# Further tokens turned ahead of the tables, gathers behind the last full table block, nine rows taken ahead of the loop

## What is computed

```python
s = einsum('bshcd,hckd->bshck', q, peer_keys)      # 8 heads, 2 halves, 128 keys
sv, si = top_k(s, 16)                              # then the best 16 of 16 x 16 sums
idx, g = expert numbers, softmax of the best 16    # 8 x 16 = 128 experts per token
act = gelu(einsum('thkd,td->thk', peer_u[it], xt)) * gt
out = einsum('thk,thkd->td', act, peer_v[it])      # 16384 experts, rows of 2048
```

## Time and profile before

| | |
|---|---|
| median of 3 runs | 3809.42 us (3808.86 to 3809.46) |
| span of the profiled execution | 3806.1 us (the page gives no other time of it) |
| PE busy | 3758.1 us, 99% |
| DVE, ACT, POOL busy | 2363.5, 1263.3, 1697.3 us |
| granted PE clock, mean | 0.996 |
| gathers' queue | 303.22 MB, 22.4% of the DMA engines' span |
| queue of SP | 492.34 MB, 35.8% |

### The profile page before, as it was taken

One profiled execution on the slowest core, in us unless ns is written; L12 is line 12 of the kernel. 1 busy time (PEld: TensorE's weight loads), 2 busy tenths in 40 slices (PEclk: granted clock), 3 DMA queues, 4 the chain that ended last, 5 costly groups with the idle time before them and its releaser, 6 DMA issues. The chain is left out here.

```text
span 3806.1 us, 56597 instructions
## 1 busy us (share of the span) xinstructions
PE 3758.1 (99%) x20173; PEld 3449.1 (91%) x20173; DVE 2363.5 (62%) x4027; ACT 1263.3 (33%) x1638; POOL 1697.3 (45%) x1449
## 2 busy tenths in 40 slices
PE   7999999999999998999999999999999999999999
PEld 5778778888888887889999999999999999999999
DVE  5382453000010207886968888888887888888887
ACT  3443453333333323224652222222222222222221
POOL 0444434444444662444015545545553555555223
PEclk9999999999999999999999999999999999999999
DMA  6223112222222322234569989889888898989777
GB/s 199 96 85 105 67 56 99 97 90 99 99 96 91 144 99 104 105 105 151 215 260 312 323 326 326 320 328 333 321 313 286 311 335 314 329 319 338 278 295 248
DMA packets 187946, 800.97 MB, mean 210 GB/s; under 512 B 21024, under 2 KB 59944, under 8 KB 134440
## 3 DMA queue, kind: packets, MB, share of 16 engines
q1 hardware_dynamic: 99776, 492.34, 35.8%
q0 software_dynamic: 83872, 303.22, 22.4%
q10 hardware_dynamic: 4184, 4.01, 0.5%
HBM read 762.39 MB, written 37.09 MB: 210 GB/s over the span
## 5 line engine op out<-in xcount | busy, mean ns | idle before, releaser
L791 ACT ACTIVATE w_hi<-ring 128x1024 fp32r<-128x1024 f32 (+1 forms) x499 | 564.5, 1136 | 1097.4 <-PE bank L1766 744.1
L637 POOL TENSOR_TENSOR p_lo<-ring,p_hi 128x512 fp32r<-128x512 f32 x432 | 563.4, 1305 | 674.3 <-ACT p_hi L791 588.7
L1766 PE MATMUL bank<-h_hi,w_hi 128*128 128x368 f32 (+1 forms) x2304 | 782.2, 339 | 16.4 <-DVE w_lo L1586 7.5
L1766 PE MATMUL bank<-h_lo,w_hi 128*128 128x368 f32 (+1 forms) x2304 | 775.8, 337 | 0.0
L1766 PE MATMUL bank<-h_hi,w_lo 128*128 128x368 f32 (+1 forms) x2304 | 775.6, 337 | 0.0
L1766 PE MATMUL bank<-act_hi,w_hi 128*128 128x368 f32 x2048 | 674.0, 329 | 0.1
L1766 PE MATMUL bank<-act_hi,w_lo 128*128 128x368 f32 x2048 | 673.9, 329 | 0.0
L1766 PE MATMUL bank<-act_lo,w_hi 128*128 128x368 f32 x2048 | 673.9, 329 | 0.0
L757 POOL DMA_INDIRECT grow<-v_rows,g_col x288 | 383.0, 1330 | 512.9 <-DVE g_acc L1621 387.3
L1586 DVE TENSOR_TENSOR w_lo<-ring,w_hi 128x1024 fp32r<-128x1024 f32 x448 | 546.2, 1219 | 81.9 <-ACT w_hi L791 62.7
L791 ACT ACTIVATE p_hi<-ring 128x512 fp32r<-128x512 f32 x464 | 292.7, 632 | 788.8 <-PE bank L1766 784.2
(11 more groups left out here) (219 smaller groups left out, 5057.7 us busy)
## 6 DMA issues: line engine op xcount, KB each, us to landing
ring<-w_exp SPq DMA_DIRECT2D x256, 1024.0 KB, 7.0
ring<-w_mix SPq DMA_DIRECT2D x64, 1024.0 KB, 4.9
tables<-wt SPq DMA_DIRECT2D x12, 2048.0 KB, 6.5
wg<-tables SPq DMA_DIRECT2D x96, 256.0 KB, 8.4
ring<-w_qk SPq DMA_DIRECT2D x20, 1024.0 KB, 4.9
ring<-w_o SPq DMA_DIRECT2D x16, 1024.0 KB, 4.9
ring<-w_pq SPq DMA_DIRECT2D x16, 1024.0 KB, 4.9
xT<-x_t SPq DMA_DIRECT2D x8, 1024.0 KB, 12.0
```

Source lines behind the costliest of these rows:

```text
L637: nc.gpsimd.tensor_tensor(p_lo[:, part, :], ring[slot][:, part, :], p_hi[:, part, :].bitcast(F32), ALU.subtract).then_inc(quarter_lo, 1)
L791: return nc.scalar.activation(out, in_, func, **kw)
L1766: return nc.tensor.matmul(out, lhsT, rhs, start=start, stop=stop)
```

## The change

1. The 16 further tokens are turned behind tile 29 (X_AFTER = 5), not in tile 44. ACT copies them to x_h and stores them itself with a DMA; x_h moves to where wt[0] will lie, so ACT waits for that store ahead of the first table copy. PE's transposes of the routes wait for x_copied.
2. Gathers no longer wait for the store of the last table: grow moves by half a KiB and its order is turned, so that grow0 and grow1 lie where only the one-hots of quarters 2 and 3 lay. DVE frees these two one quarter into the last (short) block, the other two at its end. POOL waits for nothing of x_tokens before.
3. x_tok is spread behind the first 8 turns of four rows each, that is behind row 31, not behind row 3.
4. FIRST_ROWS is (1, 2, 2, 2, 2): nine rows ahead of the loop. So three u rows are left in turn 6 instead of eight, the adds there begin two tiles sooner (14 instead of 10), LAST_ROWS sums to 16 instead of 18 and the tail has 26 instead of 28.

```diff
-TOK_AFTER, EXP_AFTER, ROUTE_AFTER = 4, 5, 6
+TOK_AFTER, X_AFTER, EXP_AFTER, ROUTE_AFTER = 4, 5, 5, 6
-TAIL_MORE = ((), (), (), (0, 3))
+TAIL_MORE = ((), (), (), ())
-FIRST_ROWS = (0, 0, 0, 2, 2)
+FIRST_ROWS = (1, 2, 2, 2, 2)
-G_TURN, T_LAST, N_TURN = 6, 5, 10
-LAST_ROWS = (1, 1, 2, 1, 1, 2, 1, 1, 2, 1, 2, 1, 0, 1, 0, 1)
+X_TURNS = 8
+G_TURN, T_LAST, N_TURN = 6, 3, 14
+LAST_ROWS = (1, 1, 1, 1, 1, 1, 1, 1, 2, 1, 2, 1, 0, 1, 0, 1)
...
-        grow = [place(f"grow{i}", 180 + 4 * i, [D // 2]) for i in range(4)]
+        grow = [place(f"grow{i}", 180.5 + 4 * ((i + 2) % 4), [D // 2]) for i in range(4)]
-        x_h = place("x_h", 188, [D])
+        x_h = place("x_h", 144, [D])
...
-            pool.wait_ge(x_copied, 4)
-            pool.dma_start(x_dram, x_h[0:NX, :]).then_inc(x_spread, 16)
-            pool.wait_ge(x_put, 32 * NS)
-            pool.wait_ge(x_spread, 16)
-            pool.wait_ge(tab_out[1], 16 * (NTB // 2))
-            pool.wait_ge(x_ready, 5)
-            pool.wait_ge(gath_free, 1)
             for b in range(2):
                 column(g_both, b, b)
-            gather(0, half_rows[0], g_both, 0)
+            with pool.Fori(0, X_TURNS) as t:
+                gather(0, half_rows[0], g_both, t)
+            pool.wait_ge(x_stored, 16)
+            pool.wait_ge(x_ready, 5)
             for k in range(NS):
                 pool.dma_start(x_tok[NX * k:NX * k + NX, :, :], x_dram.rearrange("p (a n) -> p a n", a=KC)
                                ).then_inc(x_spread, 16)
-            gather_all(0, half_rows[0], g_both, PAIRS, x_both, 1)
+            gather_all(0, half_rows[0], g_both, PAIRS, x_both, X_TURNS)
...
+                if j == X_AFTER:                                     # ScalarE, behind its part of tile 29
+                    act_e.wait_ge(x_mm, 1)
+                    for b in range(4):
+                        f(x_h[0:NX, S * b:S * b + S], bank[4 + b][0:NX, :]).then_inc(x_copied, 1)
+                    act_e.wait_ge(x_copied, 4)
+                    act_e.dma_start(x_dram, x_h[0:NX, :]).then_inc(x_stored, 16)
...
+            act_e.wait_ge(x_stored, 16)
             for b in range(2):
                 table_block(0, b, True)
...
+                    if parts < 4 and q == parts - 1:                 # VectorE, one_hots
+                        dve.sem_inc(gath_free, 2)
...
             dve.wait_ge(tab_mm, TAB_PARTS)
+            dve.sem_inc(gath_free, 2)
...
-            dve.sem_inc(gath_free, 4)
...
+                if j == X_AFTER:                                     # PE, behind tile 29
+                    pe.wait_ge(tok_copied, 4)
+                    for c in range(KC):
+                        dst = bank[4 + c // 4][0:NX, (c % 4) * P:(c % 4 + 1) * P]
+                        mm(dst, h_hi[:, c, ND:TM], ident_r[:, :], start=True, stop=False)
+                        ins = mm(dst, h_lo[:, c, ND:TM], ident_r[:, :], start=False, stop=True)
+                    ins.then_inc(x_mm, 1)
                 if j == ROUTE_AFTER:
                     pe.wait_ge(route_ok, 1)
-                    pe.wait_ge(tok_copied, 4)
+                    pe.wait_ge(x_copied, 4)
```

More of the change, by code:

```diff
@@ L384, in hybrid_block @@
             sem("acc_zero"), sem("gath_col"), sem("gath_free"), sem("gath_gelu"), sem("gath_act"))
-        x_ready, x_put, x_mm, x_copied, x_spread = (
-            sem("x_ready"), sem("x_put"), sem("x_mm"), sem("x_copied"), sem("x_spread"))
+        x_ready, x_put, x_mm, x_copied, x_stored, x_spread = (
+            sem("x_ready"), sem("x_put"), sem("x_mm"), sem("x_copied"), sem("x_stored"), sem("x_spread"))
         gath_in = [sem(f"gath_in{i}") for i in range(4)]
@@ L1152, in _ @@
                         high_half(n, n % 2, half)
[L1153 to L1156, removed]
             def expert_pair(g, turn=False):
@@ L1671, in a_u_row @@
                 if i == PAIRS - 1:
-                    dve.wait_ge(x_spread, 16 * NS + 16)
+                    dve.wait_ge(x_spread, 16 * NS)
                     dve.wait_ge(gath_free, 4 + 2 * PAIRS)
@@ L2146, in _ @@
             tables(NTB // 2 - 1, 1, False, LEFT)
[L2148 to L2155, removed]
             for n in range(R_TAB + NTB, R_V):
-                u_tile(n - E_R, n, n % 2, bank[BANK_U[n % 2]][:, 0:ND], False, x_tokens if n == R_TAB + NTB else None)
-            pe.wait_ge(x_copied, 4)
+                u_tile(n - E_R, n, n % 2, bank[BANK_U[n % 2]][:, 0:ND])
+            pe.wait_ge(tab_copied, TAB_PARTS)
             def v_product(a, c, j):
```

## The result

The changed kernel takes 3812.47 us, median of 20 runs (3808.37 to 3819.41); the kernel before, beside it, 3807.57. The ratio is 1.0016, 95% interval 1.0010 to 1.0022: some 6 us slower by the ratio, 4.9 by the medians. Forecast were 3804.8 us, and 3799.6 to 3810.5: 4.6 us less than the kernel before. The median lies outside, on the slow side. It lies in the range of rival B (3808 to 3813). The profiled span is 3814.3 us against 3806.1.

A forecast was written before the change was run, and what follows sets the result against it. PE, busy 99% of the span, was taken as the bound, so only its idle time, clock and work count. -9.3 + 4.2 + 0.5 = -4.6 us, from 3809.4 to 3804.8 us; 8 in 10 range 3799.6 to 3810.5.

The forecast's parts named there:

- rival B: x_tok at tile 63 delays a weight tile, so the stall only moves: 3808 to 3813 us, chance 0.15.
- -9.3, the old stall and its clock: First loop turn: about 7.1 us of PE idle at 2016 and the half clock behind it go, 9.3 us saved.
- the earlier gathers: Last table block: first four half rows fetched early, landing before DVE wants them; 0, at worst 0.5 us.
- +4.2, tiles 49 and 50: Nine rows ahead of the loop: PE stalls 2.5 us, plus 1.7 of half clock; bounds 0 and 10.
- +0.5, x_tok behind row 31: Near tile 63: the 1 MB of copies slows a weight load; 0.5 us lost, bounds 0 and 9.3.
- 0, the further tokens: Matmuls moved from tile 44 to behind tile 29 cost 2.0 us on either side: 0, at worst 0.5.
- Loop, turn and tail: Expert loop and tail: row counts per turn stay at 22, PE has no wait there; gain at most 0.7, taken as 0.
- A: Rival: gathers land nearer the median, so the stall goes whole without a new one; -9.3, 3800.1 us, chance 0.32.
- C: Rival: two rows per tile overload the gathers, tiles 48, 49, 50 and 53 each wait 1 to 5 us; 3818, chance 0.08.

The follow-up runs named there:

- e4: The kernel before with the eight x_tok copies issued one per four rows from row 31 on, not all behind row 3: 3800.7 us, ratio 0.9982.
- h2: e3 with the eight x_tok copies in front of row 4, as in the kernel before: 3803.5 us, ratio 0.9986.
- g2: The changed kernel with 8 idle instructions ahead of the first loop and 100 spread over turn 6: 3804.4 us, ratio 0.9992.
- f3: The changed kernel with 108 idle instructions spread behind the low halves of tiles 45 to 49, ahead of the loop: 3804.6 us, ratio 0.9996.
- g1: e3 with 28 idle instructions ahead of the first loop and 100 spread over turn 6: 3802.6 us, ratio 0.9990.
- e3: The changed kernel with the row plan of the kernel before, four rows ahead of the loop: 3799.3 us, ratio 0.9982.
- f1: The changed kernel with eight idle instructions just ahead of the first loop: 3809.8 us, ratio 1.0007.
- f4: e3 with the eight x_tok copies issued one per four rows from row 31 on, not in a block: 3800.7 us, ratio 0.9986.
- h1: The changed kernel with 108 idle instructions over turn 6 and none ahead of the first loop: 3811.8 us, ratio 1.0014.
- g4: The kernel before with 28 idle instructions ahead of the first loop and 100 over turn 6: 3809.0 us, ratio 1.0005.
- f2: e3 with twenty idle instructions just ahead of the first loop: 3811.0 us, ratio 1.0010.
- g3: e3 with 20 idle instructions spread over turn 6 and none ahead of the first loop: 3804.5 us, ratio 0.9991.

## Why the prediction was wrong

- **-9.3, the old stall and its clock: right.** Turn 0 has no gap at 2016 and its matmuls are back but ten. The prediction put it down to x_tok's new place (e4 bears that out); the earlier gathers, which it counted at 0, take most of it away too (h2).
- **+4.2, tiles 49 and 50: right within its bounds.** "PE stalls 1.8 us", taken as 2.5 with 1.7 of half clock. PE has gaps of 0.5 us more than a matmul at 1990.9 (tile 48) and 2.6 at 1999.5 (tile 49): 3.1 us, a tile sooner than worked out, and no half clock behind it:

```profile
1999.50:2002.30 2.80, 0.40 (x4) 0.10 (x2) 2.47 (x4) 2.37 (x3) 0.43 (x1) 1.00 1.04 407
2002.30:2009.00 6.70, 6.70 (x40) 6.70 (x41) 6.14 (x10) 0.00 (x0) 4.32 (x6) 1.00 0.98 371
```

  A stall of this length brings half clock in one profile and not in another (0.79 in the 6.9 us behind g2's of 3.2 us, 1.00 behind f3's of 3.1). With code in order, nine rows stand 0.0002 to 0.0014 above four (f3 and g2 against g1 and e3), 1 to 5 us: the term's size fits, but the intervals overlap.
- **+0.5, x_tok behind row 31: not contradicted.** It was issued at 2126.95, not 2115. A weight tile came late (ACT waited 11.6 us at 2152), but f1, f3 and g2 have x_tok in the same place and no PE gap there. In the four-row kernels the block falls two tiles into the next turn, with the gap of 1.1 to 4.2 us at 2182 that f4, spaced, does not have.
- **0, the further tokens: right.** PE's wait for the first one-hots is 1.9 us as in the earlier trace rows, and comes 1.7 us later, the 2.0 of the matmuls moved.
- **0, "Loop, turn and tail": the step that failed.** It said "Row counts per loop turn stay at 22" and "PE has no wait there". The counts stayed and the waits came: 13.9 us of waits in all, 15 us of PE in four turns of the profile, and 7 to 8 us in the medians (h1 against f3 and g2). The step counted work and not code. Ten instructions with their ten accumulator reads in front of the loop put its head at or next to the last place of a block, and each jump back waits for two blocks, not one. The clue was in the trace before, 5.7 us of "issue" at 2269: a pause without a gap of PE behind it, and the sum had no term for its getting longer.
- **Rivals.** A's mechanism did not happen. B's range held the result and its sign came, a wait of 5 us or more near 2130, but by luck: PE's wait at 2138 ends with a low half whose w_hi was ready at 2127.7, so no late weight tile made it, and it goes with the idle instructions and not with x_tok's place. C had the direction and a wrong reason: of tiles 48 to 53 only 48 and 49 waited.

With only the code in order, the changed kernel takes 3804.4 to 3804.6 us (g2, f3); 3804.8 was forecast. That the figures meet is partly luck, since the forecast started from 3809.4, the median of three runs, and the kernel before beside the changed one took 3807.6. As ratios, 4.6 us less are 0.9988, and g2 and f3 have 0.9992 and 0.9996, each within 0.0009. So the sum is not contradicted for the work, and it left out where the code lies. The faster kernel is e3: early tokens, early gathers, x_tok behind row 31, and four rows: 3799.3 us, 7 to 8 us under the kernel before and 13 under the changed one.

## What to carry to other kernels

Around every hardware loop read the time from the branch to the first instruction of the body, and the instruction packets at each jump: an engine that stands on "issue" there may be waiting for code, and so may one whose named releaser had ended long before. Any edit ahead of a loop, even one that adds no work inside it, can move that pause, so before an unrolled stretch is blamed or praised, run it with a few idle instructions ahead of the loop. If such a run changes the time, move the loop's head away from the last places in front of a block's edge. The trace shows whether it worked: no second wait behind the register instruction.

## What the runs showed of the hardware

- A jump back of DVE's loop waits 2.8 to 7.1 us for its head's block in turns with a DMA share of 0.87 to 0.95, and in the first loop 3.8 to 8.8 us more if the first instructions lie over an edge. With the whole body held it takes 0.3 us (first loop of f1, g1, g2 and g4).
- Shifts of 20 instructions brought more fetches (f2 in both loops, g3 in the second); 28 and 100 or 8 and 100 left none in either loop (g1, g2), and 108 in front left one a jump in the first (f3). All agree with a period of 128 instructions.
- What decides between a fetch and none seems to be how many blocks the loop lies over. The traces have about 301 DVE instructions in a turn of the first loop and 278 in one of the second, and the packets in the middle of a turn come 120 to 132 instructions apart. Take 128 to a block, and the head of the changed kernel's first loop at a block's last place. By this estimate every loop that fetched in the sixteen traces lies over four blocks, and every one that did not over three. Some 83 of 128 places would then be good for the first loop's head and 106 for the second's; no scan was made.
- The same matmuls and rows took 3799.3 us in e3 and 3811.0 in f2, which has twenty idle instructions more. The idle instructions' own time is not it: f3 has 108 and took 3804.6, less than the changed kernel, which has none.
